# Down projections of both feed-forward layers begin before the last gated k-tiles are ready; the final norm's gain row is loaded after 44 down units

## The reference, cut to what matters

```python
D_MODEL = 2048; SEQ = 256; D_FF = 5632          # D_FF / 128 = 44 k-tiles

def _swiglu(h, w_gate, w_up, w_down):
    return (jax.nn.silu(h @ w_gate) * (h @ w_up)) @ w_down

for layer in range(2):
    h = _rmsnorm(x, norm_mix[layer])
    x = x + mixer(h)                            # mLSTM + retention, then gated DeltaNet
    h = _rmsnorm(x, norm_ffn[layer])
    x = x + _swiglu(h, *ffn[layer])
return _rmsnorm(x, final_norm)
```

## Time and profile before

| what | value |
|---|---|
| median of three runs | 2955.84 us (2955.32 to 2960.12) |
| the profiled execution's own time | 2958.69 us |
| its span, first to last instruction | 2956.9 us |
| PE busy | 2854.5 us (97%) |
| PE weight load busy | 2363.4 us (80%) |
| DVE busy | 1571.3 us (53%) |
| ACT busy | 1378.2 us (47%) |
| DMA engines, mean rate | 170 GB/s |
| mean granted TensorE clock | 0.985 of full speed |

### The profile page before, as it was taken

One profiled execution on the slowest core, in us unless ns is written; L12 is line 12 of the kernel. 1 busy time (PEld: TensorE's weight loads), 2 busy tenths in 40 slices (PEclk: granted clock), 3 DMA queues, 4 the chain that ended last, 5 costly groups with the idle time before them and its releaser, 6 DMA issues.

```text
span 2956.9 us, 37031 instructions
## 1 busy us (share of the span) xinstructions
PE 2854.5 (97%) x13396; PEld 2363.4 (80%) x13396; DVE 1571.3 (53%) x1934; ACT 1378.2 (47%) x1874; POOL 115.0 (4%) x75
## 2 busy tenths in 40 slices
PE   8999989999999999999989999999999999999998
PEld 6788768888888788887878787787888888887886
DVE  4554645545445445457484757654554554554444
ACT  5444545444444344455555657454444444443443
POOL 0000000000000000002020111100000000000000
PEclk9999989999999999999999999999999999999999
DMA  7464546666666566644353535455556666665554
GB/s 236 145 189 150 150 137 187 191 189 188 190 190 186 172 189 189 197 136 135 101 157 101 155 100 157 150 150 164 187 177 202 189 191 186 190 191 178 192 192 144
DMA packets 261265, 502.74 MB, mean 170 GB/s; under 512 B 20112, under 2 KB 20368, under 8 KB 260624
## 3 DMA queue, kind: packets, MB, share of 16 engines
q1 hardware_dynamic: 259504, 494.73, 55.6%
q10 hardware_dynamic: 816, 3.15, 0.3%
q0 software_dynamic: 816, 3.15, 0.3%
HBM read 495.72 MB, written 5.24 MB: 169 GB/s over the span
## 4 chain that ended last, share of the span: by engine, by line
PE 84%; DVE 8%; ACT 4%; issue 1%; DVEq 1%; DMA 0%; ACTq 0%; SPq 0%
PE acc L545 26%; PE acc L539 25%; PE acc L540 25%; PE aux L772 4%; DVE wlo L1373 3%; PE aux L592 2%; DVE const L1720 1%; DVE arena L1758 1%; ACT whi L951 1%; DVE arena L1755 1%; DVE arena L1720 1%; DVEq L1724 0%; ACT arena L1293 0%; DVEq L1757 0%; ACT aux L1183 0%
## 5 line engine op out<-in xcount | busy, mean ns | idle before, releaser
L1373 DVE TENSOR_TENSOR wlo<-wraw,whi 128x1024 fp32r<-128x1024 f32 x928 | 1152.0, 1247 | 1149.7 <-ACT whi L951 1140.8
L951 ACT ACTIVATE whi<-wraw 128x1024 fp32r<-128x1024 f32 x928 | 974.2, 1060 | 1102.6 <-PE acc L545 1048.0
L539 PE MATMUL acc<-whi,hT_hi 128*128 128x512 f32 x2624 | 1041.5, 397 | 6.4 <-ACT whi L951 5.9
L540 PE MATMUL acc<-whi,hT_lo 128*128 128x512 f32 x2624 | 1025.7, 391 | 0.0
L545 PE MATMUL acc<-wlo,hT_hi 128*128 128x512 f32 x2624 | 709.9, 392 | 31.6 <-DVE wlo L1373 31.2
L545 PEld LDWEIGHTS acc<-wlo,hT_hi 128*128 128x128 f32 x2624 | 491.0, 188 | 149.1 <-DVE wlo L1373 48.0
L539 PEld LDWEIGHTS acc<-whi,hT_hi 128*128 128x128 f32 x2624 | 495.2, 189 | 107.7 <-issue 6.7
L540 PEld LDWEIGHTS acc<-whi,hT_lo 128*128 128x128 f32 x2624 | 495.0, 189 | 101.0 <-issue 1.0
L539 PE MATMUL acc<-whi,arena 128*128 128x512 f32 x1088 | 431.2, 396 | 13.6 <-ACT whi L951 5.1
L540 PE MATMUL acc<-whi,arena 128*128 128x512 f32 x1088 | 429.2, 394 | 0.0
L545 PE MATMUL acc<-wlo,arena 128*128 128x512 f32 x1088 | 295.6, 394 | 0.0
(11 more groups left out here) (231 smaller groups left out, 1187.7 us busy)
## 6 DMA issues: line engine op xcount, KB each, us to landing
wraw<-in_l_w_in SPq DMA_DIRECT2D x304, 512.0 KB, 3.9
wraw<-in_l_w_gate SPq DMA_DIRECT2D x176, 512.0 KB, 3.7
wraw<-in_l_w_up SPq DMA_DIRECT2D x176, 512.0 KB, 3.7
wraw<-in_l_w_down SPq DMA_DIRECT2D x176, 512.0 KB, 4.4
wraw<-in_l_w_out SPq DMA_DIRECT2D x96, 512.0 KB, 4.5
o_rounds<-arena POOLq DMA_DIRECT2D x3, 1024.0 KB, 4.7
arena<-o_rounds ACTq DMA_DIRECT2D x3, 1024.0 KB, 6.0
x<-in_x SPq DMA_DIRECT2D x4, 512.0 KB, 7.0
```

Source lines behind the costliest of these rows:

```text
L539: nc.tensor.matmul(pair[m], hi[:, k, tok], wh, start=first, stop=False)
L540: nc.tensor.matmul(pair[m], lo[:, k, tok], wh, start=False, stop=False)
L951: nc.scalar.activation(whi[:, s, :], wraw[:, s, :], ACT.Copy).then_inc(hi_done, 1)
L1373: V.tensor_tensor(wlo[:, s, :], wraw[:, s, :], whi[:, s, :].bitcast(F32), ALU.subtract).then_inc(lo_done, 1)
```

## The change

The four closing steps of `ffn` are no longer run at its end: `ffn` returns them as functions, and `residual_phase` for dn0 and dn1 calls them inside its first block, at the places that they have in an iteration of gate and up. PE transposes behind unit 3 and waits for `flo_done` behind unit 19. ACT's `f_hi` stands behind its eighth split, DVE's `up` behind its fourth and `f_lo` behind its eighth. SP's wait and the load of `fgain` move behind the loads of the first two down blocks (44 units).

```diff
@@ SyncE
+            down1 = lambda i: [(A["l1_w_down"], i * 2 * NB + b * NB) for b in range(2)]
+            phase("dn1", 2, 0, 1, down1)
             sp.wait_ge(unit_used, UNIT0["dn1"])
             sp.dma_start(fgain[:], A["final_norm"].rearrange("(a n) -> a n", a=1).to_broadcast([P, D])
                          ).then_inc(consts_in, 16)
-            phase("dn1", 2, 0, 2, lambda i: [(A["l1_w_down"], i * 2 * NB + b * NB) for b in range(2)])
+            phase("dn1", 2, 1, 2, down1)
@@ TensorE
-            def residual_phase(name, hi, lo, transposed, tiles=range(64)):
+            def residual_phase(name, hi, lo, transposed, tiles=range(64), last_f=None, last_f_in=None):
 
                 done = 4 * (NORM_OF[name] - 1)
+                f_units = lambda w: last_f_in() if last_f_in is not None and w == FKT // 2 - 3 else None
...
-                body(name, 0, 2, hi, lo, [None, xt(0, 1)], tiles=tiles)
+                body(name, 0, 2, hi, lo, [last_f, xt(0, 1)], between=f_units, tiles=tiles)
...
-                tr(FF // NB)()
-                pe.wait_ge(flo_done, n0 + FF // NB)
+                return tr(FF // NB), lambda: pe.wait_ge(flo_done, n0 + FF // NB)
...
-            ffn("gu0", "out0", 0)
-            residual_phase("dn0", fT_hi, fT_lo, True)
+            last_f = ffn("gu0", "out0", 0)
+            residual_phase("dn0", fT_hi, fT_lo, True, last_f=last_f[0], last_f_in=last_f[1])
@@ ScalarE
-            def residual_phase(name):
+            def residual_phase(name, last_f=None):
                 norm = NORM_OF[name]
 
                 def hook(i, b, j):
+                    if last_f is not None and isinstance(i, int) and i == 0 and b == 0 and j == 7:
+                        last_f()
...
-                f_hi(FF // NB)
+                return lambda: f_hi(FF // NB)
@@ VectorE
-            def residual_phase(name):
+            def residual_phase(name, last_up=None, last_f=None):
...
                 def hook(i, b, j):
                     if b == 0 and isinstance(i, int) and i == 0:
+                        if last_f is not None and j == 3:
+                            last_up()
+                        if last_f is not None and j == 7:
+                            last_f()
                         return
...
-                up(FF // NB)
-                f_lo(FF // NB)
+                return lambda: up(FF // NB), lambda: f_lo(FF // NB)
...
-            last_x_block = residual_phase("dn0")
+            last_f = ffn("gu0", "out0", last_x_block, 0)
+            last_x_block = residual_phase("dn0", *last_f)
```

More of the change, by code:

```diff
@@ L933, in _ @@
             residual_phase("out1", oT_hi, oT_lo, True, OUT1_O)
-            ffn("gu1", "out1", FF // NB)
-            residual_phase("dn1", fT_hi, fT_lo, False)
+            last_f = ffn("gu1", "out1", FF // NB)
+            residual_phase("dn1", fT_hi, fT_lo, False, last_f=last_f[0], last_f_in=last_f[1])
         @block.scalar
@@ L1150, in _ @@
             residual_phase("out0")
-            ffn("gu0", "out0", 0)
-            residual_phase("dn0")
+            last_f = ffn("gu0", "out0", 0)
+            residual_phase("dn0", last_f)
             def gdn_gates():
@@ L1351, in _ @@
             residual_phase("out1")
-            ffn("gu1", "out1", FF // NB)
-            residual_phase("dn1")
+            last_f = ffn("gu1", "out1", FF // NB)
+            residual_phase("dn1", last_f)
             last_x_block("dn1")
@@ L1675, in _ @@
             last_x_block = residual_phase("out0")
-            ffn("gu0", "out0", last_x_block, 0)
-            last_x_block = residual_phase("dn0")
+            last_f = ffn("gu0", "out0", last_x_block, 0)
+            last_x_block = residual_phase("dn0", *last_f)
             def gdn_gates():
@@ L1891, in _ @@
             last_x_block = residual_phase("out1")
-            ffn("gu1", "out1", last_x_block, FF // NB)
-            last_x_block = residual_phase("dn1")
+            last_f = ffn("gu1", "out1", last_x_block, FF // NB)
+            last_x_block = residual_phase("dn1", *last_f)
             for j in (1, 3, 4):
```

## The result

The changed kernel takes 2939.43 us in the median of six runs (2937.14 to 2942.92); the kernel before takes 2956.74 in six (2955.32 to 2960.25). The ratio is 0.9939 with a 95% interval of 0.9928 to 0.9950, so 15 to 21 us are gone. Forecast were 2940.2 us and 15.6 us.

What follows compares the result with a forecast made beforehand. PE's row of matmuls was taken as the bound, 97% busy. 7.05 us at join 1 and 8.53 at join 2 sum to 15.6, so the median goes from 2955.84 to 2940.2 us, range 2937.0 to 2946.5.

Steps and rivals of the forecast that it cites:

- Join 1: PE's hand-over from gu0 to dn0: 4.31 us idle and 2.74 us of low clock, together 7.05 us to gain.
- Join 2: PE's hand-over from gu1 to dn1: 7.07 us idle and 1.46 us of low clock, together 8.53 us to gain.
- Cover of the product: First down block: DVE's product finishes at about 982.5, PE ends unit 3 at 989.3; 7 us of cover, cost 0.
- Cover of the splits: First down block: ACT's and DVE's closing steps done by about 994, PE's wait ahead of unit 20 at 1034; cost 0.
- First down unit ready at once: At each join unit 0's splits follow the last gate-up splits directly; cost taken as 0, at most 2.3 us per join.
- loop exit free: PE leaves its gate and up loop straight into down matmuls, with no idle time hiding the branch; cost 0.
- The gain row hidden: The 1 MB fgain load in dn1's stream delays the load behind it by at most 2.6 us; cost 0 on PE.
- The clock's term: Low clock behind the pauses at both joins: 4.2 us of the gain, bounded between 0 and 5.5 us.
- 2944.5: Rival at both joins: the low clock's part does not come back, only 11.4 us of idle go; chance 0.09.
- 2948.8: Rival: dn1's first weights still late, join 2 keeps its wait, only 7.05 us go; chance 0.04 together with the gain-row rival.
- the gain row that stops the stream: Rival in dn1: fgain takes 24.8 us to land and PE waits 7.9 us, giving 2948.1; chance 0.04 together with 2948.8.
- The rival with a slower end: Without pauses PE cannot hold 2.4 GHz; one down block at 5.1 us per unit gives 2992; chance 0.02 with anything unseen.

Runs made afterwards that it cites:

- load_only: Kernel before with only the fgain load moved behind 44 down units, closing steps left at the end of gate and up; median 2953.21 us, ratio to before 0.9986.
- steps_only: Changed kernel's moved closing steps, but fgain loaded ahead of dn1's weights as in the kernel before; median 2949.34 us, ratio to before 0.9979.
- wait_early: Changed kernel with PE's wait for flo_done directly behind the transposes (behind unit 3) instead of behind unit 19; 2948.04 us in one run.
- fill_pause: Kernel before with PE's pauses at both joins filled by matmuls whose results are never read; median 2950.13 us, ratio to before 0.9978.
- out0_too: out1_too plus out0's first four units run before the retention part's norm, transposes and splits; median 2917.74 us, ratio to before 0.9870.
- out1_too: Changed kernel with the same move at l1 to out1: last gating, transposes and splits go into out1's first block; median 2927.63 us, ratio to before 0.9911.

## Why the prediction was right

- **Join 1, 7.05 us** (4.31 idle, 2.74 low clock): 7.08 between the two traces. **Join 2, 8.53 us** (7.07 and 1.46): 8.51. The prices were read from the same trace of the kernel before that stands on one side of this comparison. So the agreement shows that nothing was left of either loss and nothing new came in, and not that another execution before would have lost as much: the low clock's part varies, as below.
- **Two chains at join 2.** The prediction read from the trace that the gain row's chain ends last there, but gave no price for each part. load_only and steps_only show that each part alone is worth next to nothing at that join.
- **Cover of the product, 7 us.** PE's slot at 974.56, product finished at 977.06 + 1.41 = 978.47, transposes at 985.56: 7.1 us.
- **Cover of the splits, 40 us.** `f_lo` ends at 988.05 + 1.22 = 989.27; unit 20 begins at 974.56 + 20 x 2.75 + 0.87 = 1030.4. wait_early shows what the wait costs without the cover: 2.97 us of idle time at each join.
- **First down unit ready at once, loop exit free.** The first matmul stands 0.90 us behind the last four. The upper bound of 2.3 us per join was not needed.
- **The gain row hidden.** PE shows no wait, and ACT's splits behind the load are released by PE and not by a DMA, as this row of its timeline shows:

```profile
2793.15 1.06 ACT L953 ACTIVATE whi<-wraw 128x1024 fp32r<-128x1024 f32 x1 [1.69 <-PE acc L547]
```

  Here two details were off. The load was issued at 2782.3, 103 us into dn1 and not 115, since SP runs several units ahead of PE. And it took 8.4 us to land, not the 4.8 of the earlier trace rows. Neither reached ACT.
- **The clock's term.** The forecast took the profiled 4.2 us, with bounds 0 and 5.5. It is the clock: fill_pause removes nearly all of it (2.67 of 2.74 us at join 1; 1.09 us at join 2, where the pause became 0.27 longer) and leaves the pauses. The term for the same code varies: 2.74 us at join 1 before and 1.70 in load_only (251.24 - 245.23 - 4.31), 2.77 at join 2 of load_only behind a pause of the same length. The Trainium skill ("TensorE: Matmul & The Clock Gate", "Part 1: The HAM clock gate (the "warmup" mystery)") says of a kernel's start that the number of slow matmuls differs from run to run, with where the start falls against an observation that runs freely. The prediction applied that to a restart behind a pause; the unequal terms behind equal pauses agree with it, wait_early's two joins above all, but no run here sets where a restart falls, so the reason stays open.
- **The rivals.** The clock's part did come back and both joins were mended (1.00 at both, no pause left), so the forecasts of 2944.5 and 2948.8 are out, and so is the gain row that stops the stream. The rival with a slower end (a clock that needs pauses) is out: the 729 us without a pause stay at 1.00, and out0_too takes 2917.74 us with fewer pauses still. Between the joins the changed kernel's low stretches (from 1656, 1697, 1861 and 2005 us on) stand where the kernel before has them too, in l1 and where it ends.
- **The median.** It fell by 17.3 us and not 15.6. The interval (15 to 21 us) covers both, and the traces give no ground to credit more than 15.6 to the change. That the forecast of 2940.2 is only 0.8 us from the measured 2939.43 is partly luck: the kernel before has a median 0.9 us higher in six runs than in the three of the forecast, which hides half of the 1.7 us.
- **A slip.** Of the chances, all but the last group (0.02) were said to end faster; that is 0.98, and not the 0.96 given. Nothing rests on it.

## What to carry to other kernels

Where a phase ends in a serial tail (product, transpose, split) and the next phase reads that tail's result last, start the next phase and put the tail inside it at the places it has in a steady iteration; place the wait for the final result ahead of its first reader and not behind its producer. Price such a join as the pause plus the slow stretch that follows it, and look for a second chain that ends in the same pause (here a load behind a wait), since removing one of two gains next to nothing.

## What was not expected

- **The low clock follows pauses of 2 to 3 us only sometimes.** Two pauses of 2.97 us in one execution: 1.64 us lost behind the first, 0.03 behind the second. And it comes back differently for one place from run to run, which makes stretches that nobody touched differ: over eight profiled executions the stretch up to the slot behind gu0 took 974.25 to 978.26 us (without out0_too, which moves work there), and that from l1's first matmul to the slot behind gu1 1459.45 to 1462.23 (without out1_too as well). One such place in the kernel before and in the changed one, the same eight transposes after the same wait:

```profile
357.58 1.88 PE L592 MATMUL aux<-const,arena 128*128 128x128 f32 x8 [1.94 <-DVE arena L1528]
```

```profile
356.82 1.09 PE L594 MATMUL aux<-const,arena 128*128 128x128 f32 x8 [1.94 <-DVE arena L1535]
```

  Such places are all of the 5.3 us by which the two traces differ outside the joins. Matmul by matmul, the kernel before falls behind by 1.5 us at 129 to 133 us, 1.5 at 357 to 361 and 1.4 at 396 to 402 (and is ahead by 0.7 at 24 us): the 3.7 us of the first stretch. In l1 it loses 1.5 us at 1344 to 1348, which later waits of PE for DVE take up again, and 1.6 at 1385 to 1389, the 1.6 us of that stretch. At each of these places one execution is at the low clock and the other is not. The last of them, before and then changed, behind a wait of about 2 us (timeline, then stretch):

```profile
1385.17 2.08 PE L545 MATMUL acc<-wlo,hT_hi 128*128 128x512 f32 x4 [2.06 <-DVE wlo L1373]
...
1385.00:1389.00 4.00, 3.83 (x16) 3.45 (x17) 2.39 (x3) 0.00 (x0) 0.00 (x0) 0.57 0.66 194
```

```profile
1374.33 1.20 PE L547 MATMUL acc<-wlo,hT_hi 128*128 128x512 f32 x4 [2.07 <-DVE wlo L1377]
...
1374.00:1378.00 4.00, 3.67 (x29) 3.50 (x29) 2.54 (x3) 0.78 (x2) 0.00 (x0) 1.00 0.62 175
```

- **A broadcast row of 1 MB takes longer to land in a running stream.** 4.8 us where no weights were under way before it, 8.4 in the changed kernel's stream, 8.1 for the first of four and 14.2 for the last. A further row costs the stream only 2.6 us, so the time to landing is not the price. Why the first takes 8 us was not tried.
